# Output stage of a streaming encoder layer: a 14-place weight ring for its last five groups, 7 of 16 normalisations moved five groups later, and one set of residual rows loaded and added a group later

## The reference, cut to what matters

```python
y_ssm = _rmsnorm(y_ssm, ssm_ng)          # (rows, 1024), rows: 1024 prompt, 64 sample
y_att = _rmsnorm(o * silu(z_att), att_ng)  # (rows, 1024)
y = jnp.concatenate([y_ssm, y_att], axis=-1)
x = x + (y @ w_out)                      # w_out (2048, 2048), everything float32
```

## Time and profile before

| | |
|---|---|
| median of 3 runs | 1949.09 us |
| the profiled execution | 1948.71 us, of which the span of instructions 1947.1 us |
| granted TensorE clock, mean over the span | 0.996 |
| PE busy | 1903.2 us (98%) |
| DVE, ACT, POOL busy | 1138.3, 709.5, 439.1 us |
| output stage | from 1580.94 us to the end of the span |

### The profile page before, as it was taken

One profiled execution on the slowest core, in us unless ns is written; L12 is line 12 of the kernel. 1 busy time (PEld: TensorE's weight loads), 2 busy tenths in 40 slices (PEclk: granted clock), 3 DMA queues, 4 the chain that ended last, 5 costly groups with the idle time before them and its releaser, 6 DMA issues.

```text
span 1947.1 us, 32969 instructions
## 1 busy us (share of the span) xinstructions
PE 1903.2 (98%) x11368; PEld 1777.1 (91%) x11368; DVE 1138.3 (58%) x2189; ACT 709.5 (36%) x1395; POOL 439.1 (23%) x756
## 2 busy tenths in 40 slices
PE   5999999999999999999999999999999999999988
PEld 4899999999999999999999999999999987888767
DVE  7855665556454554645546455464575658665654
ACT  6422333333232334333343333433354443433331
POOL 5874445556112002020010200102001010100111
PEclk9999999999999999999999999999999999999999
DMA  8344443444325314133142331413347454432554
GB/s 202 120 115 113 110 111 103 115 128 120 100 64 169 98 48 138 57 106 97 46 138 57 106 97 46 139 56 107 100 142 242 145 186 134 157 103 97 187 189 149
DMA packets 212055, 230.50 MB, mean 118 GB/s; under 512 B 33978, under 2 KB 167188, under 8 KB 210772
## 3 DMA queue, kind: packets, MB, share of 16 engines
q1 hardware_dynamic: 185392, 143.58, 26.1%
q0 software_dynamic: 21072, 74.93, 11.5%
q10 hardware_dynamic: 5524, 11.14, 1.6%
HBM read 166.83 MB, written 62.74 MB: 118 GB/s over the span
## 4 chain that ended last, share of the span: by engine, by line
PE 92%; DVE 4%; DMA 2%; ACT 1%; SPq 1%; issue 0%; POOL 0%; DVEq 0%; ACTq 0%
PE GB L195 61%; PE TB L2329 3%; PE TB L2350 3%; PE TB L2461 3%; PE TB L2462 3%; PE TB L2463 3%; PE GB L2461 2%; PE GB L2462 2%; PE GB L2463 2%; PE TB L2371 2%; PE TB L1137 1%; PE TB L2390 1%; PE GB L1058 1%; PE TB L1147 1%; PE TB L1148 1%; PE TB L1041 1%
## 5 line engine op out<-in xcount | busy, mean ns | idle before, releaser
L195 PE MATMUL GB<-XH,whi 128*128 128x384 f32 x2448 | 827.7, 338 | 0.8 <-ACT QR L1723 0.8
L195 PE MATMUL GB<-XH,wlo 128*128 128x384 f32 x2448 | 800.6, 327 | 0.0
L195 PE MATMUL GB<-XL,whi 128*128 128x384 f32 x2448 | 798.0, 326 | 0.0
L195 PEld LDWEIGHTS GB<-XH,whi 128*128 128x128 f32 x2448 | 459.9, 188 | 14.0 <-issue 8.8
L183 DVE TENSOR_TENSOR wlo<-wraw,whi 128x256 fp32r<-128x256 f32 x412 | 201.2, 492 | 457.1 <-ACT whi L179 452.0
L195 PEld LDWEIGHTS GB<-XL,whi 128*128 128x128 f32 x2448 | 460.2, 188 | 5.3 <-issue 3.8
L195 PEld LDWEIGHTS GB<-XH,wlo 128*128 128x128 f32 x2448 | 459.3, 188 | 0.0
L179 ACT CAST whi<-wraw 128x256 fp32r<-128x256 f32 x412 | 166.5, 405 | 645.8 <-PE GB L195 635.1
L2072 DVE RECIPROCAL SQ<-SQ 128x136 f32<-128x136 f32 x128 | 127.5, 996 | 1.4
L1770 ACT ACTIVATE PR<-PR,nmx 128x128 f32<-128x128 f32 (+8 forms) x72 | 53.4, 742 | 183.8 <-DVE nmx L2043 171.7
L1677 ACT CAST AREAR<-AREA 128x512 fp32r<-128x512 f32 x86 | 53.0, 620 | 145.6 <-DMA AREA<-t_s 80.6
(11 more groups left out here) (487 smaller groups left out, 2808.3 us busy)
## 6 DMA issues: line engine op xcount, KB each, us to landing
wraw<-in_w_in SPq DMA_DIRECT2D x380, 128.0 KB, 2.2
TS<-in_w_out POOLq DMA_DIRECT2D x32, 512.0 KB, 5.8
t_s<-TS POOLq DMA_DIRECT2D x16, 1024.0 KB, 4.8
AREA<-in_w_out SPq DMA_DIRECT2D x44, 256.0 KB, 3.5
AREA<-t_s SPq DMA_DIRECT2D x42, 256.0 KB, 2.7
AREA<-in_x_prompt POOLq DMA_DIRECT2D x32, 256.0 KB, 4.9
out_y_prompt<-AREA POOLq DMA_DIRECT2D x28, 256.0 KB, 3.5
wlof<-t_s SPq DMA_DIRECT2D x22, 256.0 KB, 2.7
```

Source lines behind the costliest of these rows:

```text
L195: ins = T.matmul(group(GB if bank is None else bank, b), w[:, s % SPL, kk], x[:, k + kk, c:c + n], start=first and kk == 0 and i == 0, sto ...
```

## The change

It has three parts.

1. From piece 72 (the first of group 9) the ring has 14 places: 8 new ones in the lower half of `XH`, whose quarters are used up by then, and the 6 old ones. The first 8 of these loads wait until the last quarter there has been read (`alo`, `mix_s4`); after that a load waits for the piece 14 before it. Also from piece 72 on ACT and DVE run 3 pieces further ahead: high parts up to `n + 7`, low parts up to `n + 6`. The wait for the low part of piece `n - 4` stays.
2. In group 0 DVE runs 9 norms and not 16: both halves of attention tile 7, and half 1 of tiles 0 to 6. Half 0 of tiles 0 to 6 is normalised in group 5, where 8 of the 16 mixes leave for group 6. The counts of `mix` follow. The load of group 1's residual rows waits for the first two norms, not for all 16.
3. The residual rows of c21 for group 12 are loaded after those of c12 for group 11, not before, on semaphore `x_in0`; they are added at pieces 4 and 5 of group 12, not of group 11. The take of group 11 now waits until all eight of these transfers have landed.

```diff
@@ constants and ring
-LEAD_HI, LEAD_LO = 4, 3
+LEAD_HI, LEAD_LO, LEAD_WIDE = 4, 3, 3
...
             RING = ORING + 2
+            WIDE, NWIDE = KG * 9, 8
+            FULL = RING + NWIDE
...
-            def mix_ya(k):
-                return 2 * k + 2
+            def mix_q22(k):
+                return 1 if k == KG - 1 else k + 3
...
+            def mix_q12(k):
+                return 2 if k == KG - 1 else 43 + 2 * k
...
             def out_slot(n):
 
-                i = n % RING
+                j = (n - WIDE) % FULL if n >= WIDE else FULL
+                if j < NWIDE:
+                    return tuple(a[:, 1024 * j + NW * x:1024 * j + NW * (x + 1)] for a, x in ((XHR, 0), (XHR, 1), (XHFF, 1)))
+                i = (WIDE + j - NWIDE if n >= WIDE else n) % RING
...
+            def out_before(n):
+
+                if n < WIDE + NWIDE:
+                    return n - RING if n < WIDE else None
+                return n - RING - NWIDE
@@ SP, out_load
+                    elif out_before(n) is None:
+                        sp.wait_ge(f["alo"], stands["alo"] + opnd_at(S1, KG - 1))
+                        sp.wait_ge(f["mix"], stands["mix"] + mix_s4(KG - 1))
                     else:
-                        out_freed(sp, n - RING)
+                        out_freed(sp, out_before(n))
@@ POOL
-                pool.wait_ge(f["mix"], stands["mix"] + mix_ya(KG - 1))
+                pool.wait_ge(f["mix"], stands["mix"] + mix_q12(KG - 1))
...
                 sample_out("sr", 10, o0)
-                residual("c21", 12, UU[0], x1)
                 pool.wait_ge(o0, 288)
                 residual("c12", 11, BX[0], x0)
+                residual("c21", 12, UU[0], x0)
@@ ACT
-                    while done <= min(n + LEAD_HI, len(PIECES) - 1):
+                    while done <= min(n + LEAD_HI + (LEAD_WIDE if n >= WIDE else 0), len(PIECES) - 1):
@@ DVE
                     if m == 5:
-                        dve.wait_ge(f["x_in0"], 288 + 64 * c)
+                        dve.wait_ge(f["x_in0"], 288 + 128 * c)
...
-                    dve.wait_ge(f["x_in1"], 160 + 64 * c)
+                    dve.wait_ge(f["x_in1" if c else "x_in0"], 160 if c else 416)
...
-                    while done <= min(n + LEAD_LO, len(PIECES) - 1):
+                    while done <= min(n + LEAD_LO + (LEAD_WIDE if n >= WIDE else 0), len(PIECES) - 1):
...
                     if g == 0:
-                        for k in ((0, 1, 2), (3, 4, 5), (6, 7))[i - 5]:
-                            norm(1, k, 0)
+                        for k in ((KG - 1, 0), (1, 2, 3), (4, 5, 6))[i - 5]:
                             norm(1, k, 1)
+                            if k == KG - 1:
+                                norm(1, k, 0)
@@ DVE, groups 5 and 6
                         mix(quarter(0, i, 1), quarter(0, i, 1), quarter(1, i, 1), ALU.add, mix_s2(KG - 1))
-                        mix(quarter(1, i, 0), quarter(1, i, 0), quarter(1, i, 1), ALU.subtract, mix_s2(KG - 1))
-                    if g == 6 and i:
-                        opnd_lo(S1, 1, i - 1, quarter(0, i - 1, 1))
+                        if i < KG - 1:
+                            norm(1, i, 0)
+                    if g == 6:
+                        if i:
+                            opnd_lo(S1, 1, i - 1, quarter(0, i - 1, 1))
+                        mix(quarter(1, i, 0), quarter(1, i, 0), quarter(1, i, 1), ALU.subtract, mix_q12(i))
...
-                    if g in (11, 13) and i in (4, 5):
+                    if g in (12, 13) and i in (4, 5):
                         for t in (2 * i - 8, 2 * i - 7):
-                            residual_c21(g // 13, t)
+                            residual_c21(g - 12, t)
```

More of the change, by code:

```diff
@@ L1259, in attention @@
             TMP = wraw[0:DEC, 2:4].rearrange("p a b c -> p (a b c)")
-            XLR, XLFF = (a[:].rearrange("p k t -> p (k t)") for a in (XL, XLF))
+            XHR, XHFF, XLR, XLFF = (a[:].rearrange("p k t -> p (k t)") for a in (XH, XHF, XL, XLF))
             def opnd(a, which, k, low):
@@ L1292, in opnd_at @@
                 return KG * which + k + 1
-            def mix_ya(k):
-                return 2 * k + 2
+            def mix_q22(k):
+                return 1 if k == KG - 1 else k + 3
             def mix_q11(k):
-                return 17 + k
+                return 10 + k
             def mix_q21(k):
-                return 25 + 2 * k
+                return 18 + 2 * k
             def mix_s3(k):
-                return 26 + 2 * k
+                return 19 + 2 * k
             def mix_s2(k):
-                return 41 + k
+                return 34 + k
             def mix_s1(k):
-                return 49 + 2 * k
+                return 42 + 2 * k
+            def mix_q12(k):
+                return 2 if k == KG - 1 else 43 + 2 * k
             def mix_s4a(k):
-                return 50 + 2 * k
+                return 57 + k
             def mix_s4(k):
@@ L1871, in scalar @@
                             out_freed(act, piece_at(9, KG - 1))
-                        opnd_hi(1, i, quarter(1, i, 1), mix_ya(i))
+                        opnd_hi(1, i, quarter(1, i, 1), mix_q22(i))
                     if g in (3, 4) and i < 2:
```

## The result

The changed kernel takes 1928.7 us, the median of 4 runs (1928.16 to 1930.57), against 1949.01 us for the kernel before (4 runs): the ratio is 0.9898, with a 95% interval of [0.9884, 0.9912]. That is 20.3 us less, where 17.6 were forecast (1931.5) and the range ended at 1929.8. In the first profile the direction and the end of every wait came out as forecast; the size was too small by 2.8 us, and the time lies 1.1 us under the range. The profiled execution took 1928.19 us with a span of 1926.6 us.

A forecast was written before the change was run, and what follows sets the result against it. PE was taken to be the bound, 98% busy, with only its output-stage waits and slow-clock stretches to win. 13.3 idle + 2 x 1.7 clock + 6 x 0.16 = 17.7 us off, plus a tenth for thin margins: 1931.5 us, range 1929.8 to 1937.

The forecast's parts named there:

- All of PE's six waits go: Output stage, groups 1 and 10 to 12: six PE waits ending on DVE, 13.3 us in all, disappear.
- The norms: 2.6 us: Fewer norms in group 0 let DVE's first take finish in time, removing PE's group 1 wait: 2.6 us, margin 0.2.
- The norms' new places in groups 5 and 6: Groups 5 and 6: norms replace mixes, eight mixes move on; DVE has idle time to cover them, cost nothing.
- The ring: 9.5 us: Groups 10 to 12: earlier place release removes the 5.1 us wait with its clock dip and smaller waits, 9.5 us together.
- part 3: 5.7 us: Group 11: later residual rows remove DVE's 7.45 us stand and PE's 3.8 us wait with its clock dip, 5.7 us.
- the 3.8 us wait: PE wait mid group 11, blamed on DVE standing 7.45 us before L2175 for residual rows with low parts queued behind.
- Take of group 11 late: Rival: group 11's take waits for eight transfers; slower landings make PE wait 1 to 5 us, 1932.5 to 1938; chance 0.12.
- Sixth accumulator, margin 0.3 us: Start of group 11: the third take ends at 1855.6, before PE needs its bank at 1855.9.
- the terms for clock and idle time, 2 x 1.7 + 13.3: Output stage: PE's six waits, 13.3 us idle, plus two slow-clock stretches of 1.7 us each after the long waits.
- The low end of the range: Whole kernel: 1929.8 us, allowing for 1.7 us, one clock dip less.

The follow-up runs named there:

- norms_residual: Changed kernel with the 14-place ring and larger leads turned off, moved norms and later residual rows kept: 1945.53 us, ratio 0.9978 to the kernel before.
- no_lead: Changed kernel with 14 places but the old leads (high parts to n + 4, low parts to n + 3): 1930.38 us, ratio 0.9900 to the kernel before.
- ring_only: Kernel before plus only the 14-place ring and larger leads, norms and residual rows as before: 1932.93 us, ratio 0.9921.
- residual_only: Kernel before plus only c21's residual rows loaded after c12's and added in group 12: 1947.4 us, ratio 0.9988.
- ring10: Changed kernel with 10 ring places in place of 14, leads as changed: 1940.25 us, ratio 0.9952 to the kernel before.
- norms_only: Kernel before plus only the norms moved out of group 0, ring and residual rows as before: 1946.13 us, ratio 0.9981.

## Why the prediction was wrong, point by point

- *All of PE's six waits go.* Right: none left in the first profile of the changed kernel, one of 0.7 and one of 1.2 us in the next two.
- *The norms: 2.6 us, by a margin of 0.2.* Right, and alone too: group 1 28.2 to 25.6 us. The margin is as thin as I said: group 1 is 25.9 us in norms_residual and 26.0 in no_lead, there with a wait of 0.2 us for this take.
- *The norms' new places in groups 5 and 6 cost nothing.* Right: 21.76 us each.
- *The ring: 9.5 us, and part 3: 5.7 us.* The sum fits the two first profiles (group 10 1.1, group 11 12.4, group 12 1.8, in all 15.3 us against 15.2), the split is not right. I gave the 3.8 us wait to the instruction that stood in DVE's queue. The ring covers that stand by itself (ring_only: DVE idle for 10.0 us, no wait of PE behind it), and part 3 alone gains about 2 us (residual_only), since a weight load behind the same transfers is late as well. With the ring, part 3 takes a wait of about 1 us in group 12.
- *Take of group 11 late*: it was not. The collision behind the eight transfers is real, but it hits the weight loads. It costs PE 4.5 and 4.3 us with six places (residual_only, norms_residual) and 4.0 with ten (ring10), and nothing with 14.
- *Sixth accumulator, margin 0.3 us*, priced with the norms' margin at a tenth. That was the next wait: 0, 0.7 and 1.2 us in three profiles. Group 11 of the changed kernel is 30.2 us in their mean, 1.0 over the 29.2 that I gave it, which took back part of what the longer waits of the kernel before added to the gain.
- **The step that failed**: the terms for clock and idle time, 2 x 1.7 + 13.3, were read from one execution and taken for the kernel's own. Measured in four more profiles, group 11 is 0.5 to 2.4 us longer than in that one: the 3.8 us wait is 4.6 us in the mean of all five, and the clock costs 3.1 to 5.1 us where the term has 3.4. At the same time I set the sum against a total whose start was the latest of 18, which hid that its stage was the shortest of five. Between the means the stage fell by 19.3 us, where the sum has 17.7, and 0.4 more lie in front of it. The low end of the range allowed 1.7 us for a slow stretch less in the changed kernel, but not for longer ones in the kernel before.
- **How much of the miss that explains**: of the 2.8 us about two, 1.6 in the stage and 0.4 in front of it. That the two first profiles give 18.0 us for the stage, so near to 17.7, is in part luck: both stages are the shortest of their kind. The 0.6 us between profiles and medians stays open.

## What to carry to other kernels

A long wait of TensorE (here 3.8 us and more) can cost its idle time and then a stretch of slow clock whose length changes from one execution to the next; when such waits are to go, price the stretch from several profiles, or put the whole spread into the range. When two waits lie close together, ask of each part of a change what it does alone: a deeper ring covered a stall that seemed to need a new order, and the new order without the ring mostly moved the stall. Before trusting a total, compare a landmark that the change can't reach, such as the start of the stage, between the two traces.

## What was not expected of the hardware

- The start of the output stage moved by 2.1 us among four profiles of one and the same program (1578.85 to 1580.94), and by 3.3 us over all 18. In the latest of them the lateness was there 61 us into the program.
- Two runs of twenty one-column matmuls, 2.1 us each, were followed in 15 of 16 profiles by one or two slow stretches of TensorE's clock (about 1.7 or 3.3 us lost) though no row shows TensorE idle there; spread among full-width matmuls they were followed by none in two profiles.
- Every wait of 3.8 us and more in the output stage came with a slow stretch of the clock, in all nine profiles that have such waits (the five of the kernel before's work, norms_only, residual_only, norms_residual, ring10); waits up to 2.4 us did not.
